# Writing out the inner loops over an expert's chunks on PE, ACT and DVE

## What is computed

```
def swiglu(h, w_gu, w_down):
    g, u = jnp.split(h @ w_gu, 2, axis=-1)
    return (jax.nn.silu(g) * u) @ w_down

def moe_swiglu(h, w_router, w_gu, w_down):
...
    for e in range(N_EXPERTS):
        out = out + gate[:, e:e + 1] * swiglu(t, w_gu[e], w_down[e]).astype(jnp.float32)
```

## Time and profile before

| | us |
|---|---|
| median of 3 runs | 2044.43 |
| lowest, highest | 2042.71, 2044.49 |
| the profiled execution, first to last instruction (span) | 2045.7 |
| PE busy (matmul), share of the span | 1832.3, 90% |
| DVE busy | 1418.0, 69% |
| ACT busy | 1076.0, 53% |

### The profile page before, as it was taken

How to read it: one execution, slowest core, us unless ns; L and a number is a source line. 1 busy time by engine, 2 the same in 40 slices (tenths; PEclk the granted TensorE clock), 3 DMA queues, 4 the chain that set the end, 5 groups by cost and what they waited for, 6 DMA issues and landing times.

```text
span 2045.7 us, 23915 instructions
## 1 busy us (share of the span) xinstructions
PE 1832.3 (90%) x7877; PEld 1397.8 (68%) x7877; DVE 1418.0 (69%) x1378; ACT 1076.0 (53%) x989; POOL 28.2 (1%) x42
## 2 busy tenths in 40 slices
PE   6696878899989967776899999999999999999997
PEld 4553456688877534655688777787777878778776
DVE  5356467544465473753788888888888888888886
ACT  3222434444434223341677676776776767767674
POOL 2100000000000000000000000000000000000000
PEclk8798989899999989986899999999999999999999
DMA  7831256255534213540699899998999989989894
GB/s 217 251 100 62 78 185 185 89 194 179 184 137 152 98 62 97 185 144 1 226 359 366 295 364 324 327 366 298 364 324 327 366 295 364 353 300 365 297 365 166
DMA packets 341384, 481.25 MB, mean 235 GB/s; under 512 B 15260, under 2 KB 270044, under 8 KB 340832
## 3 DMA queue, kind: packets, MB, share of 16 engines
q1 hardware_dynamic: 338224, 467.62, 67.2%
q0 software_dynamic: 2720, 12.02, 2.8%
q10 hardware_dynamic: 400, 1.08, 0.1%
HBM read 477.26 MB, written 3.41 MB: 235 GB/s over the span
## 4 chain that ended last, share of the span: by engine, by line
PE 72%; DVE 12%; ACT 6%; issue 4%; DMA 3%; DVEq 2%; ACTq 0%; SPq 0%
PE ps L476 21%; PE ps L478 21%; PE ps L477 20%; PE ps L541 2%; PE ps L730 2%; PE ps L738 2%; DMA raw<-in_w_in 1%; DVE w_lo L360 1%; ACT w_hi L800 1%; ACT scratch L1248 1%; PE ps L688 1%; DVE x_sb L887 1%; ACT w_hi L355 1%; DVE w_lo L850 1%; DMA raw<-in_w_xkv 1%
## 5 line engine op out<-in xcount | busy, mean ns | idle before, releaser
L476 PE MATMUL ps<-w_hi,hT_hi 128*128 128x512 f32 x1488 | 616.1, 414 | 80.3 <-DVE hT_lo L467 30.6
L478 PE MATMUL ps<-w_lo,hT_hi 128*128 128x512 f32 x1488 | 598.1, 402 | 0.0
L477 PE MATMUL ps<-w_hi,hT_lo 128*128 128x512 f32 x1488 | 597.7, 402 | 0.0
L850 DVE TENSOR_TENSOR w_lo<-raw,w_hi 128x2048 fp32r<-128x2048 f32 x168 | 384.9, 2291 | 62.7 <-ACT w_hi L800 62.7
L850 DVE TENSOR_TENSOR w_lo<-z,w_hi 128x2048 fp32r<-128x2048 f32 x169 | 386.5, 2289 | 58.6 <-ACT w_hi L800 58.0
L476 PEld LDWEIGHTS ps<-w_hi,hT_hi 128*128 128x128 f32 x1488 | 285.9, 192 | 159.3 <-DVE w_lo L360 39.0
L800 ACT ACTIVATE w_hi<-z 128x2048 fp32r<-128x2048 f32 x169 | 323.0, 1914 | 45.8 <-PE ps L478 41.0
L800 ACT ACTIVATE w_hi<-raw 128x2048 fp32r<-128x2048 f32 x168 | 321.0, 1911 | 24.4 <-PE ps L478 24.4
L478 PEld LDWEIGHTS ps<-w_lo,hT_hi 128*128 128x128 f32 x1488 | 285.5, 192 | 69.2
L477 PEld LDWEIGHTS ps<-w_hi,hT_lo 128*128 128x128 f32 x1488 | 286.4, 192 | 62.4 <-issue 1.9
L360 DVE TENSOR_TENSOR w_lo<-raw,w_hi 128x2048 fp32r<-128x2048 f32 (+1 forms) x89 | 194.6, 2195 | 142.2 <-ACT w_hi L355 141.7
(11 more groups left out here) (238 smaller groups left out, 1174.1 us busy)
## 6 DMA issues: line engine op xcount, KB each, us to landing
z<-in_w_gu_moe SPq DMA_DIRECT2D x224, 512.0 KB, 5.0
raw<-in_w_gu_moe SPq DMA_DIRECT2D x224, 512.0 KB, 5.2
z<-in_w_down_moe SPq DMA_DIRECT2D x114, 512.0 KB, 5.1
raw<-in_w_down_moe SPq DMA_DIRECT2D x112, 512.0 KB, 5.1
raw<-in_w_in SPq DMA_DIRECT2D x80, 512.0 KB, 4.6
raw<-in_w_gu_dense SPq DMA_DIRECT2D x44, 512.0 KB, 4.6
raw<-in_w_down_dense SPq DMA_DIRECT2D x22, 512.0 KB, 4.0
raw<-in_w_xkv SPq DMA_DIRECT2D x16, 512.0 KB, 4.6
```

The source lines that it names most:

```text
L476: pe.matmul(acc, a, wh, start=start and j == 0, stop=False)
L477: pe.matmul(acc, b, wh, start=False, stop=False)
L478: ins = pe.matmul(acc, a, wl, start=False, stop=stop and last)
L850: v.tensor_tensor(w_lo[:, moe_ring(p), :], moe_raw(p), w_hi[:, moe_ring(p), :].bitcast(F32), ALU.subtract) \
```

## The change

The loops L760 (PE) and L793 (ACT and DVE) become Python loops, so that the instructions of all chunks of a pass stand in the program one after the other. The loops over pairs stay. The order of the work, the buffers and the waits' values are the same; SP's program is not touched. The arguments that `moe_order` no longer needs go.

```diff
@@ pe_moe
                     pe.wait_ge(sem("x_added"), n)
                     pe_gather(pe, n + 1)
-                    with pe.Fori(3, N_MOE) as c:
+                    for c in range(3, N_MOE):
                         pe_moe_chunk(pe, ip, par, c)
@@ moe_order
-        def moe_order(split, act_of, aT_of, hook, ip, par, fori):
+        def moe_order(split, act_of, aT_of, hook):
...
-            with fori(2, N_MOE // 2) as u:
+            for u in range(2, N_MOE // 2):
                 chunk(u, 0)
                 chunk(u, 1)
@@ act_moe
-                    moe_order(split, silu, aT, hook, ip, par, act.Fori)
+                    moe_order(split, silu, aT, hook)
@@ dve_moe
-                    moe_order(split, gated, aT, hook, ip, par, v.Fori)
+                    moe_order(split, gated, aT, hook)
```

## The result

The changed kernel takes 2051.94 us (median of 20 runs, 2043.35 to 2061.61) against 2045.45 us for the kernel before (20 runs, 2041.66 to 2052.80). The ratio is **1.0025, 95% interval 1.0013 to 1.0037**: slower by some 5 us. I had forecast no measurable change, 2044.0 us.

The account below looks back on a forecast made before the run. PE was taken to bound the expert stage. Loop control -0.7, fetches ahead of use +0.3 and the fetch at the branch back 0 gave -0.4 us, from the median 2044.43 to 2044.0 us, range 2042.5 to 2053.

Parts of the forecast that it names:

- (b): PE's instruction fetch at the branch back over a pair, taken three times: 0 us forecast, 3.0 us the upper end.
- cover: At PE's branch back, the 4.2 us until DVE delivers act_done, during which a fetch would cost nothing.
- the sign: Chunk times at the three branches back stay near 9.95 us; moves over 0.5 us each would refute the prediction's reason.
- rival 2: At PE's branch back, the fetch outlasts its 4.2 us wait; at 6.5 us a fetch, 2051 us; 8%.
- The first term: Loop control removed in second experts of the four pairs: -0.7 us, 0.9 us at most.
- Term (a): Instruction packets fetched ahead of use in the straight code: 0.3 us added, 2.4 us the upper bound.
- the count of packets: PE's instruction queue q8 would bring about ten packets a pair from 1160 us on.
- rival 1: At branch back L824, ACT's and DVE's bodies no longer stay and are refetched: 2052 to 2059 us; 15%.
- Rival 4: PE starves on fetch inside straight code; 0.2 us late for each of 40 packets gives +8 us, 2052 us; 4%.
- Rival 3: Loop control was dearer, or ACT's two table reloads at the pair loop's head go: -4.2 us for the latter, 2039.8 us; 5%.

Follow-up runs that it names:

- e8: The changed kernel with each transfer of the expert stage bringing a quarter of its bytes; 2048.18 us in a single run.
- e4: The changed kernel run once more, nothing altered; 2052.45 us, ratio 1.0031.
- e6: The changed kernel with one Silu ahead of ACT's loop over pairs, so that ACT's two table reloads at its head go; 2051.72 us, ratio 1.0032.
- e2: The changed kernel with PE's loop kept, only ACT's and DVE's loops written out; 2043.02 us, ratio 0.9989.
- e1: The kernel before with only PE's loop written out, ACT's and DVE's loops kept; 2049.22 us, ratio 1.0019.
- e11: The changed kernel with a prefetch hint for PE's branch L750 and one Silu ahead of ACT's loop over pairs; 2039.87 us, ratio 0.9965.
- e7: The changed kernel with PE's loop kept and one Silu added ahead of ACT's loop over pairs; 2040.79 us, ratio 0.9984.
- e3: The changed kernel with PE's loop written out only in a pair's first expert, about 1,620 PE instructions; 2043.50 us, ratio 0.9988.
- e9: The changed kernel with PE's loop kept for the second expert's last 8 chunks, about 1,940 PE instructions; 2050.72 us in a single run.

## Why the prediction was wrong

**The step that failed is (b)**, the fetch at the branch back. I put it at 2.8 to 5.2 us, from a small transfer's landing and that of a load in this stage, took it as hidden under 4.2 us of cover, and allowed 1.0 us a branch at most. It takes 5.7 to 6.6 us. Two things were in that: an instruction fetch at a branch has no row to be compared with in the kernel before, and costs 4 us even with the DMA engines mostly free (e8), more than the 2.8 us of the small transfer; and I chose the lower bound "as nearer" where the DMA share of 0.98 should have sent me to the upper one or past it. The range for a resource that no row shows, on engines that are never free, should have gone beyond the slowest load. The prediction had named the sign: its reason is wrong if the heads move by over 0.5 us each, and they moved by 1.9, 3.2 and 2.7. This was rival 2, priced at 2051 us for 6.5 us a fetch, with 8%. Its mechanism and place are what happened; its chance was far too small. That 2051 is so near to the 2051.94 measured is partly luck: the fetches alone give 5.3 us where it had 6.9; the clock, which it did not have, adds 2.5, and the loops' end takes 1.6 off.

**The consequence that no case had** is the clock: a stall of 2.5 to 3.7 us can be followed by 3.4 to 6.8 us at half clock. It is some 2.5 of the 7.8 us in the first profile and more in e4. From the rows: at the first branch back PE resumes at 1234.97, 2.2 us after act_done; the chunk grows by 1.9 us. At the second the chunk grows by 3.2 us with a branch longer by only 0.2 us.

**The cover itself was right.** It held a fetch of 4.1 us in e8 without a trace, and without the cover nothing changed for the later of the two (e6).

**The first term was too small.** I took -0.7 us for the loop control, with 0.9 as the most, from the 0.23 us in nine chunks. ACT's and DVE's half gives 2.1 us (e2). The 0.04 us places vanished in all four second experts, and they are worth 0.7 us, as I had taken. But the same experts also lost 0.16 us each (0.4 in the first pair) in the chunk after the gather, 13.49 to 13.33 us, 0.9 us in all, and the three chunks at the branch back 0.16 us each, 9.94 to 9.78; 0.2 us went back in the stage's first chunk. I had measured only the nine regular chunks and not compared the others of the two experts. Its cause was half right: PE's loop control has a share in it (e1).

**Term (a) was right**: fetches ahead of use cost nothing to be seen, 0.3 us in a stage with ten packets a pair (e11 against e7), and these lie in the stage's first chunk. So was the count of packets (ten a pair and one at the branch, 36 from 1160 us on); that ACT's and DVE's bodies stay (rival 1 did not come: q14 is silent after the first pass); that the reloads of tables stay at the head of the pair loop; and what each case would look like in the trace, the idle put down to "issue" among it. Rival 4 did not come. Rival 3's price for the tables was nearly right: I said 4.2 us for three heads; e7 gives 1042.7 - 1038.3 = 4.4 us, of which 0.6 us are in the first chunk of the stage (9.20 to 8.63), so 3.8 us for the three.

The page "Runtime: NRT & Kernel Launch" of the Trainium skill gives PE a buffer of 2,048 instructions in its section on instruction fetch mechanics, and says that a taken branch to code outside its current two blocks forces a fetch. The runs bear out the fetch (5.7 to 6.6 us), not the two blocks: e3's body of seven packets stays. The limit that matters lies under 1,940 instructions (e9). The same section gives this as a reason why kernels prefer full unrolling; here it went the other way, as writing out made the branch fetch where the loop had not.

## What to carry to other kernels

Before writing out a loop inside another, count the outer body's instructions, not the inner one's gain: on PE 1,620 stayed and 1,940 did not, and from there each taken branch back took 5.1 to 6.6 us under full DMA. If the body must be longer, hint the branch (it then takes 0.4 us); else leave the loop on the engine whose loop control is hidden anyway and write out the others' (e2). And read the stage, not the span: here the span moved the other way, as the stage began 9.6 us earlier behind the same work, and a regular part of a loop does not speak for its ends.

## What the runs showed that I had not expected

- A taken branch to code that is not held costs PE 5.1 to 6.6 us with DMA share 0.98 and 3.8 to 4.1 us with 0.28; with a hint 0.34 to 0.40 us; held, 0.21 us. The load of the DMA engines acts by how long the packet waits to start: 3.1 to 4.0 us in the changed kernel, 1.2 to 1.8 us with light loads.
- The half clock behind a stall of 2.5 to 3.7 us lasts 0, 3.4 or 6.8 us, in one and the same kernel. It has a part in the wider spread of the changed kernel's times (2043 to 2062 us, before 2042 to 2053), but not the larger one in its two profiles: their spans differ by 12.6 us, 9.0 of them ahead of the stage and 3.6 in it. Where the part ahead of the stage comes from stays open.
- ACT's table loads at a loop's head come from two paths with different tables that meet there. One activation ahead of the loop, with one load of its own, took away eight of 1.28 us each and, with the fetch out of the way, 4.4 us.
